# A decoder layer in f32 on one core: how the sampled rows' cached values are multiplied, and where those products stand

## What is computed

```python
z = rms_norm(x) @ w_in                      # q, k, v (3 groups x 4 heads x 64), GLU, two gates
a = merged window attention of three groups # (window, dilation) = (128,1), (512,4), (2048,16)
cb = silu(layer_norm(causal_dwconv(u))) @ w_conv_out
h = sigmoid(ga) * (a @ w_att) + sigmoid(gb) * cb
x = x + h @ w_out
x = x + swiglu(rms_norm(x))
```

```python
kg = ext_k[:, idx]; vg = ext_v[:, idx]      # ext = cache rows, then the 4 new rows
s = einsum('bshd,bsjhd->bshj', q, kg) * ATT_SCALE
o = einsum('bshj,bsjhd->bshd', softmax(s), vg)
```

## Time and profile before

| | |
|---|---|
| median of three runs | 1867.36 us |
| the three runs | 1859.78, 1867.36, 1868.85 us |
| the profiled execution | 1867.65 us, its span 1865.9 us |
| TensorE matmul busy | 1780.9 us, 95% of the span |
| VectorE, ScalarE, GpSimd busy | 1046.3, 458.9, 69.9 us |
| mean granted clock of TensorE | 0.968 |
| the tiles' products, line 962 | 50.7 us busy, 288 records |

### The profile page before, as it was taken

How to read it: one execution, slowest core, us unless ns; L and a number is a source line. 1 busy time by engine, 2 the same in 40 slices (tenths; PEclk the granted TensorE clock), 3 DMA queues, 4 the chain that set the end, 5 groups by cost and what they waited for, 6 DMA issues and landing times.

```text
span 1865.9 us, 25207 instructions
## 1 busy us (share of the span) xinstructions
PE 1780.9 (95%) x10357; PEld 1671.8 (90%) x10357; DVE 1046.3 (56%) x1464; ACT 458.9 (25%) x900; POOL 69.9 (4%) x125
## 2 busy tenths in 40 slices
PE   6999989999999988989998999999999999999999
PEld 5899989999988888979987789899899899899897
DVE  5688988788987766585304432424424424424425
ACT  5111122323433554512102232121121121121120
POOL 0000000000000011110110000000000000000000
PEclk9999999999999999999579999999999999999999
DMA  6111233234242357865524002222222222222232
GB/s 190 53 60 56 94 120 115 91 114 152 94 138 90 134 168 246 286 212 192 188 78 147 1 34 91 91 91 91 91 91 91 91 91 90 91 90 90 92 109 103
DMA packets 156486, 211.54 MB, mean 113 GB/s; under 512 B 9090, under 2 KB 127010, under 8 KB 155603
## 3 DMA queue, kind: packets, MB, share of 16 engines
q1 hardware_dynamic: 145971, 134.01, 23.3%
q0 software_dynamic: 10416, 76.16, 10.9%
HBM read 180.04 MB, written 74.80 MB: 137 GB/s over the span
## 4 chain that ended last, share of the span: by engine, by line
PE 85%; DVE 6%; DMA 3%; DVEq 2%; SPq 1%; issue 1%; ACT 1%; ACTq 0%; POOL 0%; POOLq 0%
PE ps L694 19%; PE ps L695 19%; PE ps L696 19%; PE ps L1137 4%; PE ps L1135 4%; PE ps L1136 4%; PE ps L962 2%; DVE conv L1498 2%; PE ps L1059 2%; PE ps L1061 2%; PE ps L1060 2%; PE ps L908 1%; DMA qb<-scr_q 1%; PE ps L782 1%; SPq L482 1%
## 5 line engine op out<-in xcount | busy, mean ns | idle before, releaser
L694 PE MATMUL ps<-xhi,whi 128*128 128x352 f32 x1200 | 405.8, 338 | 8.6 <-DVEq L1553 7.0
L696 PE MATMUL ps<-xhi,wlo 128*128 128x352 f32 x1200 | 388.2, 323 | 0.0
L695 PE MATMUL ps<-xlo,whi 128*128 128x352 f32 x1200 | 388.1, 323 | 0.0
L694 PE MATMUL ps<-nhi,whi 128*128 128x352 f32 x1056 | 341.3, 323 | 0.0
L695 PE MATMUL ps<-nlo,whi 128*128 128x352 f32 x1056 | 339.0, 321 | 0.0
L696 PE MATMUL ps<-nhi,wlo 128*128 128x352 f32 x1056 | 338.6, 321 | 0.0
L1498 DVE SCALAR_TENSOR_TENSOR conv<-u,vec,conv 128x1024 f32<-128x1024 f32 x240 | 308.4, 1285 | 25.6 <-issue 11.1
L1454 DVE TENSOR_TENSOR wlo<-raw,whi 128x1024 fp32r<-128x1024 f32 x126 | 153.6, 1220 | 249.4 <-ACT whi L1225 241.2
L694 PEld LDWEIGHTS ps<-xhi,whi 128*128 128x128 f32 x1200 | 228.4, 190 | 19.3 <-DVEq L1553 7.6
L695 PEld LDWEIGHTS ps<-xlo,whi 128*128 128x128 f32 x1200 | 228.7, 191 | 4.2
L696 PEld LDWEIGHTS ps<-xhi,wlo 128*128 128x128 f32 x1200 | 228.0, 190 | 0.0
(11 more groups left out here) (214 smaller groups left out, 2085.1 us busy)
## 6 DMA issues: line engine op xcount, KB each, us to landing
kv_sample<-cache_kv_w POOLq DMA_DIRECT2D x32, 1022.0 KB, 6.5
raw<-w_in SPq DMA_DIRECT2D x50, 512.0 KB, 4.6
raw<-w_gate_up SPq DMA_DIRECT2D x44, 512.0 KB, 3.8
scr_z<-zt SPq DMA_DIRECT2D x34, 528.0 KB, 3.2
qb<-scr_q POOLq DMA_DIRECT2D x24, 512.0 KB, 5.6
raw<-w_down SPq DMA_DIRECT2D x22, 512.0 KB, 4.2
kc<-cache_kv_w POOLq DMA_DIRECT2D x16, 512.0 KB, 6.9
vc<-cache_kv_w POOLq DMA_DIRECT2D x16, 512.0 KB, 4.3
```

What stands on the lines that cost most here:

```text
L694: pe_mm(out, wh, rhs_hi, start=first, stop=False)
L695: pe_mm(out, wh, rhs_lo, start=False, stop=False)
L696: return pe_mm(out, wl, rhs_hi, start=False, stop=last)
```

## The change

The cached values become the moving operand, and the probabilities the weights. For each sequence and sampled token one product moves the 256 values of 128 positions, all four heads' at once, through 32 columns of weights. These 32 columns stand for the 2 sequences x 4 tokens x 4 heads of a pair of sequences; all but the 4 (or, in group 0, 16) that belong to this product are zero. So 8 x 1 + 16 x 4 = 72 products add up in bank 7, now with one row for each sequence, token and head, and all four heads' channels in it, of which only the row's own head is wanted.

GpSimd prepares the zero-padded weights `ptz` and `ptz0` (`spread_probs`) behind the loads of the first three tiles. `new_values` gives its own 64 channels in bank 6. On VectorE, `sample_rows` picks each row's own head out of bank 7 with a mask (`rowhead`) and adds it, in six operations; TensorE turns the result once (`sample_turn`), and from there `sample_hi` and `sample_lo` go on as before. `ptz` takes the room of two more tiles of x, so five of the eight now load behind `s_pv`, and `nfw` behind the turn.

`VTILES` now puts no tile behind any of the 16 `att` units and eight behind each of `out` 0, 1 and 2.

```diff
+    ptz = at("ptz", [P, 2, NS, 32], F32, S3 + (KT - 5) * D * 4)
+    ptz0 = at("ptz0", [P, DEC_B, 32], F32, S3 + KT * D * 4)
...
-    VTILES = [0] * 3 + [1] * 13 + [4, 4, 3]
+    VTILES = [0] * 16 + [8, 8, 8]
...
-        for t in range(KT - 3):
+        for t in range(KT - 5):
             residual_load(t)
         att_gate_load(2)
         sp.wait_ge(s_pv, 1)
+        for t in range(KT - 5, KT):
+            residual_load(t)
+        sp.wait_ge(s_oT2, 1)
         sp.dma_start(nfw[:, :], a["norm_ffn_w"].partition_broadcast(P).rearrange("q a d -> q (a d)")).then_inc(s_nfw, 16)
-        for t in range(KT - 3, KT):
-            residual_load(t)
         ffn_load(FFN0 + 1)
...
+        def spread_probs():
+
+            nc.gpsimd.memset(ptz[:, :, :, :], 0.0)
+            nc.gpsimd.memset(ptz0[:, :, :], 0.0)
+            pool.wait_ge(s_ptr, 1)
+            pool.drain()
+            for par in range(2):
+                for g in range(1, NG):
+                    to, of = ptz[:, g - 1, DEC_S * par, 16 * par:16 * par + 4], ptr[:, g, 0, 16 * par:16 * par + 4]
+                    nc.gpsimd.tensor_copy(bass.AP(to.tensor, to.offset, [to.ap[0], [2 * DEC_S * 32, 4], [32 + NH, DEC_S], [1, NH]]),
+                                          bass.AP(of.tensor, of.offset, [of.ap[0], [32, 4], [NH, DEC_S], [1, NH]]))
+                last = nc.gpsimd.tensor_copy(ptz0[:, par:DEC_B:2, 16 * par:16 * par + 16],
+                                             ptr[:, 0, 0, :].rearrange("p (x r) -> p x r", r=16)[:, par:DEC_B:2, :])
+            last.then_inc(s_pz, 1)
...
             cache_tile(vc[n % 3], s_kc[n % 3], 1, n % NG, n // NG)
+            if n == 2:
+                spread_probs()
...
             if n == 0:
-                pe.wait_ge(s_ptr, 1)
+                pe.wait_ge(s_pz, 1)
                 pe.wait_ge(s_oTl, 5)
             pe.wait_ge(s_kc[n % 3], 16 * ((NB + n) // 3 + 1))
+            dst = ps[32 * (b // 2):32 * (b // 2) + 32, 7, 0:GW]
             for s in range(DEC_S if g else 1):
-                w = NH if g else NH * DEC_S
-                col = b * NH * DEC_S + s * NH
-                for hp in range(2):
-                    mm = nc.tensor.matmul(ps[:, 7, hp * P + col:hp * P + col + w], vc[n % 3][:, s if g else DEC_S - 1, hp * P:(hp + 1) * P],
-                                          ptr[:, g, 0, col:col + w], start=n == 0 and hp == 0 and s == 0, stop=False, skip_group_check=True)
+                w = ptz[:, g - 1, DEC_S * b + s, :] if g else ptz0[:, b, :]
+                mm = nc.tensor.matmul(dst, w, vc[n % 3][:, s if g else DEC_S - 1, :], start=b % 2 == 0 and g == 0,
+                                      stop=b % 2 == 1 and g == NG - 1 and s == DEC_S - 1, skip_group_check=True)
             mm.then_inc(s_kcf, 1)
...
             for g in range(NG):
-                for hp in range(2):
-                    mm = nc.tensor.matmul(ps[:, 7, hp * P:(hp + 1) * P], rowv[:, g, :, :].rearrange("p a d -> p (a d)"), ptr[:, g, 1, :],
-                                          start=False, stop=g == NG - 1, skip_group_check=True)
+                mm = nc.tensor.matmul(ps[:, 6, 0:HD], ptr[:, g, 1, :], rowv[:, g, 0, :], start=g == 0, stop=g == NG - 1)
             mm.then_inc(s_pv, 1)
+
+        def sample_turn():
+            pe.wait_ge(s_orow, 1)
+            nc.tensor.transpose(ps[:, 6, P:2 * P], orow[:, :, :].rearrange("p a d -> p (a d)"), ident[:, :]).then_inc(s_oT2, 1)
...
+            if r == V_END + 1:
+                sample_turn()
...
         def sample_hi():
-            act.wait_ge(s_pv, 1)
+            act.wait_ge(s_oT2, 1)
...
+        V.tensor_reduce(rowhead, ident[:, :].rearrange("p (x h) -> p h x", h=NH), AX_X, ALU.add)
...
+        def sample_rows():
+
+            dve.wait_ge(s_pv, 1)
+            V.tensor_copy(orow[:, 0, :], ps[:, 6, 0:HD])
+            for h in range(NH):
+                dve.drain()
+                V.scalar_tensor_tensor(orow[:, 0, :], ps[:, 7, h * HD:(h + 1) * HD], rowhead[:, h:h + 1], orow[:, 0, :], ALU.mult, ALU.add)
+            dve.drain()
+            V.tensor_copy(orow[:, 1, :], orow[:, 0, :]).then_inc(s_orow, 1)
...
                 residual(0, i)
+                if r == V_END:
+                    sample_rows()
```

More of the change, by code:

```diff
@@ L214, in build @@
     vc = [at(f"vc{i}", [P, DEC_S, GW], F32, S3 + (KT - 3 + i) * D * 4) for i in range(3)]
+    ptz = at("ptz", [P, 2, NS, 32], F32, S3 + (KT - 5) * D * 4)
+    ptz0 = at("ptz0", [P, DEC_B, 32], F32, S3 + KT * D * 4)
+    assert (KT * D + DEC_B * 32) * 4 <= REG and 2 * NS * 32 == 2 * D
+    orow = at("orow", [P, 2, HD], F32, o_band + 3 * P * 4)
+    rowhead = rs9[:, 12:16]
     x1s = at("x1s", [NS, D], F32, WO[0] + 2 * KT * 512 * 4)
@@ L261, in build @@
     s_qb = [sem(f"s_qb{i}") for i in range(2)]
-    s_prod, s_sc, s_row, s_rowT, s_rowt, s_snew, s_prow, s_pexp, s_ppT, s_ptr, s_pv, s_kcf, s_osh, s_osl = (
-        sem(n) for n in ("s_prod", "s_sc", "s_row", "s_rowT", "s_rowt", "s_snew", "s_prow", "s_pexp", "s_ppT", "s_ptr", "s_pv", "s_kcf", "s_osh", "s_osl"))
+    s_prod, s_sc, s_row, s_rowT, s_rowt, s_snew, s_prow, s_pexp, s_ppT, s_ptr, s_pv, s_kcf, s_osh, s_osl, s_pz, s_orow, s_oT2 = (
+        sem(n) for n in ("s_prod", "s_sc", "s_row", "s_rowT", "s_rowt", "s_snew", "s_prow", "s_pexp", "s_ppT", "s_ptr", "s_pv", "s_kcf", "s_osh", "s_osl", "s_pz", "s_orow", "s_oT2"))
     s_o12, s_cd, s_cw, s_comb, s_oT, s_oTh, s_oTl = (sem(n) for n in ("s_o12", "s_cd", "s_cw", "s_comb", "s_oT", "s_oTh", "s_oTl"))
@@ L1386, in sample_hi @@
         def sample_hi():
-            act.wait_ge(s_pv, 1)
+            act.wait_ge(s_oT2, 1)
             for h in range(NH):
                 r = slice(HD * (h % 2), HD * (h % 2) + HD)
-                src = ps[r, 7, (h // 2) * P:(h // 2 + 1) * P].rearrange("p (x h) -> p x h", h=NH)[:, :, h]
+                src = ps[r, 6, P:2 * P].rearrange("p (x h) -> p x h", h=NH)[:, :, h]
                 last = act.copy(othi[r, h // 2, SEQ:T], src)
```

## The result

| | before | after |
|---|---|---|
| median of five runs | 1863.78 us | 1848.87 us |
| the runs, lowest to highest | 1859.78 to 1868.85 us | 1847.73 to 1850.66 us |
| the profiled execution | 1867.65 us | 1850.66 us |
| from the first `att` unit to the 17th | 111.3 us | 92.0 us |
| ahead of it and behind it, in the span | 876.6 + 878.0 us | 876.7 + 880.3 us |

The ratio on record is 0.9908, with a 95% interval from 0.9887 to 0.9929; the two medians alone give 0.9920. So the change is faster by 0.8 to 0.9%, which is 15 to 17 us.

A forecast was written before the change was run, and what follows sets the result against it. TensorE was taken as the bound, half of this stretch at 1.2 GHz. The terms sum to 91.0 us in place of 111.3; less 20.3, plus 0.2, from the profiled 1867.65 us gives 1847.5 us, range 1839 to 1859.

The forecast's parts named there:

- 16 `att` units: Units in a row without tiles, held to VectorE's pace of 1.483 us each: 18.0 us until `out` 0.
- three `out` units: `out` 0 to 2 on TensorE at full clock, 5.57 us each: 16.7 us.
- the products at full clock: The tiles' 72 products of 256 f32 columns on TensorE, 0.427 us each at 2.4 GHz: 30.7 us.
- waits for tiles: TensorE waits in the blocks for buffer refills, six times 2.5 us: 15 us, between 13 and 20.
- new values: Three products of two records at 107 ns on TensorE: 0.65 us.
- `out` 3: The `out` unit behind the new values on TensorE: 5.57 us.
- the turn: Behind `out` 3, TensorE waits for transpose, copies, subtractions and three hand-offs: 2.4 us.
- The clock after waits: In the blocks, one or two of six waits make TensorE's clock fall: 2 us, between 0 and 6.
- rival 1: Tile bursts in the blocks run at 1.2 GHz: 1867 us; chance 0.08 in full, 0.06 by half (1857).
- Rival 2: The clock falls already among the `att` units and stays low: slower, 1882 us; chance 0.05.
- GpSimd: `spread_probs`, behind the third load at 879.2 and wanted at 900.2, has up to 21 us free: costs 0.
- Rival 3: Loads of x for t = 3 late (1852.5 us) or GpSimd's `spread_probs` slow (1857.5 us); chance 0.05.

The follow-up runs named there:

- the order alone: Kernel before with only the new VTILES (no tiles behind the 16 att units, eight behind each of out 0, 1, 2), old products: 1863.61 us, ratio 0.9992.
- the 32 moving columns: Changed kernel's order and zero-padded probabilities, but values again as 128-column weights and 32 probability columns moving: 1863.50 us, ratio 0.9979 to the kernel before.
- the products alone: Changed kernel with the old VTILES (one tile behind each of units 3 to 15, then 4, 4, 3): 1855.59 us, ratio 0.9941 to the kernel before.
- the last experiment: Changed kernel with early GpSimd copy and tiles spread between att units (1844.46 us), GpSimd's drain between memsets and copies replaced by a semaphore: 1837.08 us.

## Why the prediction was right, point by point

The 91.0 us of the sum stand against 92.0 measured:

| step | predicted | measured |
|---|---|---|
| 16 `att` units | 18.0 | 18.0 (894.65 - 876.65) |
| three `out` units | 16.7 | 17.3 |
| products, waits, clock falls in the blocks | 47.7 | 48.3 (14.7 + 16.4 + 17.2) |
| of this, the products at full clock | 30.7 | 31.1 (144 x 0.216) |
| of this, waits for tiles | 15, six | 14.6, ten |
| new values | 0.65 | 0.69 |
| `out` 3 | 5.57 | 5.66 |
| the turn | 2.4 | 2.0 |

**The cause.** The mechanism held: the clock is low under the narrow products and stays up where 256 columns move. Three kernels bear it out: the order alone gives nothing, the 32 moving columns next to nothing (0.2%), and the products alone keep 0.95. "At equal clock the old records cost as much" held too, though both sizes were a little off: by the distance of two starts at full clock it is 288 records at 112 ns before and 144 at 216 after, so 32.3 and 31.1 us, where I had 107 and 213.

**How much of the number was luck.** I had taken my 20 us off the profiled execution of 1867.65 us. The median of five of before is 1863.78, and from there the same sum gives 1843.7, 5 us below what was measured, though still inside my range. Of the 20 us forecast the two profiles show 17.0: the stretch gave 19.3, and the part behind it took 2.3 back. So the mechanism and the stretch were right, and the last microseconds of agreement are chance.

**VectorE's pace.** On VectorE the `att` units follow each other as in the backlog of the earlier trace rows, at 880.68, 882.16 and on, 1.483 us each. So VectorE bound these 18 us, and `out` 0 came within 0.05 us of the forecast. Only where GpSimd's copies run, near 890, is one interval 1.54.

**The waits.** The total was right, the pattern wrong: I had one wait of 2.5 us for every three tiles, there are ten from 0.56 to 2.45. The first wait of a block is as forecast (2.13, 2.01, 2.45); it then shifts the later loads, so that a second and a third tile are each a little late. The total stays: in the first block the last tile's load is issued when the fifth tile ends (909.25) and the tile starts at 913.24, so the middle wait of 0.93 only makes the last one shorter.

**The clock after waits.** One of the ten waits, 1.96 us at 933.29, cost the clock (ten records in 4.03 us where 2.3 would do; the block is busy for 11.88 us where the first, with as many records, is for 10.19); the others, up to 2.45 us, did not. That is inside my 0 to 6, and rival 1 did not come: two of the three blocks are at 1.00 between their waits. The Trainium skill, TensorE: Matmul & The Clock Gate, "HAM oscillation — how this bites in real kernels", tells of bursts of some 2 us that each start at the low clock behind a wait for a DMA; its waits are longer than any here, and here nine of ten bursts did not start low. Rival 2 did not come either: 16.68 us busy of 18.0 at 1.00 (this counts overlapping records; going by starts, TensorE works 0.98 of each 1.483 us).

**GpSimd.** I took 0, and 0 it was, but not for want of a cost. The preparation took from 879.15 to 891.8, of which its own work is some 4 us; 12.7 us of the 21 us of cover were used up. The term was at nothing because the order hides it, and in every order that wants a tile early it is the whole question, up to 11 us. I had looked at the instructions and passed over the drain between them. The estimate of 4 us for the elements, from the Trainium skill, GPSIMD Engine Reference, "Elementwise — side-by-side cycle accounting", agrees in its total only: the memsets of 2304 elements took 2.1 us, the copies of 384 took 1.7. The Trainium skill, GPSIMD Engine Reference, "Instruction dispatch", puts some 6 us on the first call to a freshly loaded kernel, which no run shows: the part paid once is some 2.5 us, the larger part is the drain's wait.

**The turn and x.** 2.0 against 2.4; the five loads of x behind `s_pv` landed in time, and nothing waited for them. Rival 3 did not come.

**Behind the stretch.** I had assumed that all behind the 17th `att` unit takes what it took. It took 2.3 us more, 880.3 instead of 878.0. The waits there are the same or shorter, 3.83 us for 4.20 and 2.82 for 2.82, but the clock falls longer. TensorE's windows of before at the first of them:

```profile
1003.98:1008.98 5.00, 3.42 (x8) 0.66 0.49 123
1008.98:1013.98 5.00, 5.00 (x23) 1.00 1.07 412
```

and of after there, and at the wait of 2.82 us, behind which it stayed at 1.00 before:

```profile
984.35:989.35 5.00, 3.44 (x8) 0.55 0.44 120
989.35:994.35 5.00, 5.00 (x18) 0.77 1.05 410
1009.35:1014.35 5.00, 2.38 (x6) 0.78 0.01 3
1014.35:1019.35 5.00, 5.00 (x20) 0.88 0.00 0
```

Over all profiles here this rest runs from 877.4 us (the last experiment) to 880.5, for the same instructions. Which of two equal waits costs the clock, and why, stays open; it put the profiled execution at 1850.66 where the stretch alone would have given 1848.3. The median of five, 1848.87, lies 1.4 above the forecast.

## What to carry to other kernels

A matrix engine that is busy all the time can still run at half clock. It did here where it loaded 128 columns of weights to move 4 to 32 columns, and exchanging the operands so that the wide one moves paid, even at the price of multiplying by zeros. Then read every drain or other fence on an engine that also issues loads, and replace it with a semaphore on the very instructions that matter. Once both are done, put the work into the gaps of the engine that another one paces, rather than into blocks that outrun their buffers.

## What was unexpected of the hardware

- A drain on GpSimd behind its own loads let nothing through until they had landed, 8.4 to 9.2 us behind the last value load's issue, and 2.8 to 2.9 us more where it was the engine's first; without the drain the same copies began 0.14 us behind the memsets.
- The same length of wait, even at the same instruction, keeps the clock in one kernel and loses it in another (2.82 us: 1.00 before, 0.78 and 0.88 after).
- Where tiles and `att` units alternate at full clock, a unit and a tile of four products take 3.00 us (902.52 to 905.52 in the products alone), 0.3 more than 0.98 + 1.73. What the difference is was not tried.
